# A mixture-of-experts layer: shared expert weights kept resident, one list product per step, and half a shared product moved behind the first up product

## The chip, the cores and the metric

The kernel runs on one core of one Trainium2 chip. The metric is the device time of one execution in microseconds. The engines are named as in the profile: PE (TensorE), DVE (VectorE), ACT (ScalarE), POOL (GpSimd), SP (SyncE, which here only issues DMAs). Each executes its own instructions in order and waits on semaphores.

## The reference

One decoder layer over 512 tokens of width 1024, everything in float32 unless the kernel lists token numbers. After the mixers and the output projection the residual stream is x. Then:

```
h2  = rmsnorm(x, g_ffn)
idx, wts = route(h2, w_router, router_bias)      # sigmoid scores, top 8 of 64, group-limited
moe = routed_experts(h2, idx, wts, w_exp_gate, w_exp_up, w_exp_down) \
    + swiglu(h2, w_sh_gate, w_sh_up, w_sh_down)  # the shared expert: 1024 -> 256 -> 1024
x   = x + moe
x   = x + sigmoid(rmsnorm(x, g_ple) @ w_ple_gate) * rmsnorm(p @ w_ple_proj, g_ple_post)
```

Each of the 64 experts has gate and up matrices of 1024x256 and a down matrix of 256x1024, 3 MB in all; the 64 together are 192 MB of the 301 MB that the kernel moves.

## The kernel before

The tokens are four tiles of 128. The first third of the kernel computes the mixers. The gates of the mixers lie in the buffer `gates`, whose upper half `hi` (8 KB a partition for the router's weights and more) is free once `merged_ready` has counted to 8. Weights go through `ring`, 12 slots of 1 MB.

In the middle stage (263 to 349 us in the trace) PE makes the output projection (`out_proj`), transposes x (`second_T`), computes the router's logits (`router`), and ranks each token among those of its expert (`rank`). DVE selects the experts (`select`) and builds `place`, bf16 one-hot matrices that say which token stands in which slot of an expert's list. ACT writes the normed rows h2 to HBM in four stores (line 900). POOL gathers them from there by the lists, 128 rows a step, with indirect DMAs (`gather`, line 759); it starts when the stores have landed (`act_moved`) and the first list is there (`rows_listed`).

The expert loop has `STEPS` = 40 steps of 128 slots. Experts are sorted by how many tokens they have and taken in groups of four: the first 8 groups have 96 slots an expert, so 3 steps a group, the other 8 have 64, so 2 steps. Step r does, on PE: `up(r)` (64 matmuls, line 2105), the transposes of the activations of r-1, the transposes of the gathered rows of r+1 (`rows_T`, line 1654), a round of lists `lists(r)` for the next groups as long as r < 16, jobs of the shared expert, and `down(r-1)` (line 2134). ACT and DVE each copy half of the transposed rows to `hgT` (lines 933 and 1472; for step 0 ACT copies both, lines 964 and 933), ACT applies silu (938), DVE multiplies (1477). The order in each engine's queue is the order in which the program is written.

A round of lists multiplies each 128x128 block of `place` by two small matrices in separate chains of matmuls: by `tokc` (token number, 2 columns, line 1987) and by `tokw` (weight in three bf16 parts and a rank for two experts, 8 columns, line 1994).

SP issues all weight loads in one order. A slot is loaded again when the product that reads it is done: `in_used(step)` waits for `gu_ps`, `down_used(step)` for `y_ps`. In a group of three steps the third up product frees two experts' gate and up slots at once. Expert 3's gate and up weights go to slots 6 and 7.

The shared expert is computed for tiles 0 and 1 in the middle stage (`shared_up`, line 1931, in pieces that fill PE's waits; the last piece, k = 4 to 8 of tile 1, stands behind `rows_T(0)` and ahead of `up(0)`), and for tiles 2 and 3 in steps 24 to 26 (`late_up`, lines 1917 and 1920). Its gate and up weights are loaded to slots 6 and 7 for the first two tiles, and again to `hi` and a piece of `lo`, the lower half of `gates`, for the other two (lines 547 and 549). Up product 1 writes the PSUM bank of tile 1's shared product, so it waits for `shared_act` to be 2.

Of the kernel before, what the change touches and what calls it, by code (L numbers as in the profile page):

```python
# [55 lines left out]
LCOL = TCOL + 2 * WCOL  # L56
# [76 lines left out]
def alibi_table():  # L133
# [17 lines left out]
    ["wa0", "wb0", "wa1", "wb1"] + [f"out{c}" for c in range(4)] + ["shg", "shu"]  # L151
DENSE_SLOT = [u % 8 for u in range(17)] + [1, 2, 3, 4, 6, 7]
# [25 lines left out]
def build(nc, t, y_dram, h2_dram, out):  # L178
    ctx = ExitStack()
    with ctx:  # L180
# [46 lines left out]
        prow = hi[:, 2 * D:3 * D].rearrange("p (i n) -> p i n", i=NT)  # L227
        rw = hi[:, 3 * D:3 * D + KD * NE].rearrange("p (k e) -> p k e", k=KD)
        gffn = hi[:, 0:D]
        sh_row = hi[:, 0:NT * FE].rearrange("p (i f) -> p i f", i=NT)  # L230
# [4 lines left out]
        lo3 = lo[:, 3 * D:4 * D]  # L235
        rows3 = rows[:, 3, :]
        shg_late = hi[:, 2 * D:4 * D].rearrange("p (k n) -> p k n", k=KD)
        shu_late = [w.rearrange("p (k n) -> p k n", k=KD // 2) for w in (lo3, hi[:, D:2 * D])]
        choice, masked, repl, gscr = (hi[:, D + k * NR:D + (k + 1) * NR] for k in range(4))
# [13 lines left out]
        WM = NR * WCOL // 2  # L253
# [13 lines left out]
        idT = sb("idT", [P, P], BF16)  # L267
# [48 lines left out]
        mid_loaded, late_loaded, sh_late_loaded = sem("mid_loaded"), sem("late_loaded"), sem("sh_late_loaded")  # L316
# [41 lines left out]
        def unit_source(name):  # L358

            w_in = t["w_in"][0].rearrange("(p k) n -> p k n", k=KD)  # L360
            c0 = {"q0": 512, "q1": 768, "kv": 1024, "pool0": 0, "pool1": 256}
            if name in c0:
                return w_in[:, :, c0[name]:c0[name] + 256]
            n = int(name[-1]) if name[-1].isdigit() else 0
            if name.startswith("gate"):
                return t["w_gate"][0].rearrange("(p k) n -> p k n", k=KD)[:, :, n * 256:(n + 1) * 256]
            if name[:2] in ("wa", "wb"):
                w = t["w_branch_a" if name[1] == "a" else "w_branch_b"][0]
                return w.rearrange("(k p) n -> p k n", p=P)[:, :, n * 512:(n + 1) * 512]
            if name.startswith("out"):  # L370
                return t["w_out"][0].rearrange("(k p) n -> p k n", p=P)[:, :, n * 256:(n + 1) * 256]
            if name == "shg":
                return t["w_sh_gate"][0].rearrange("(k p) n -> p k n", p=P)
            if name == "shu":
                return t["w_sh_up"][0].rearrange("(k p) n -> p k n", p=P)
            raise ValueError(name)
# [78 lines left out]
        def _(sp):  # L455
# [28 lines left out]
            for u in range(8, DENSE_AT["shg"]):  # L484
                load_dense(u)
# [3 lines left out]
            for u in range(DENSE_AT["shg"], N_DENSE):  # L489
                load_dense(u)  # L490
# [4 lines left out]
            sp.dma_start(rbias, t["router_bias"].broadcast_to([P, NE])).then_inc(mid_loaded, 16)  # L495

# [339 lines left out]
        def _(act):  # L836
# [187 lines left out]
        def _(dve):  # L1024
# [33 lines left out]
            nc.vector.tensor_copy(idT[:, :], cst[:, C_ID:C_ID + P])  # L1058
# [253 lines left out]
            nc.vector.tensor_copy(tokc[:, :, 1], cst[:, C_TILE:C_TILE + NT])  # L1312
            residual(0, 0)
# [98 lines left out]
            link(nc.vector.tensor_copy(tw3[:, :, 0], r_w))  # L1412
            link(nc.vector.tensor_tensor(rest, r_w, tw3[:, :, 0], ALU.subtract))
            link(nc.vector.tensor_copy(tw3[:, :, 1], rest))
            link(nc.vector.tensor_tensor(rest, rest, tw3[:, :, 1], ALU.subtract))
            nc.vector.tensor_copy(tw3[:, :, 2], rest)
# [10 lines left out]
            nc.vector.tensor_scalar(tokw[:, :, :, 3], count_of[:, b, :, HEAD:], -1.0, None, ALU.add  # L1427
                                    ).then_inc(tokw_ready, 1)
            shared_mult(1)


            def weights_of(g, found):
# [4 lines left out]
                w = found[:, :, TCOL:].rearrange("p s (e c) -> p s e c", e=2)  # L1437
# [72 lines left out]
            for r in range(STEPS):  # L1510
                if r:
                    act_T(r - 1, (r - 1) % 2)
                act_rows(r, r % 2)
                if r + 1 < STEPS:
                    rows_T(r + 1, (r + 1) % 2)
                if 1 <= r < NGROUP:
                    dve.wait_ge(list_ps, r + 1)
                    rows_of(r, found_of(r))
                    if r == 1:
                        weights_of(0, found_of(0))  # L1520
                    weights_of(r, found_of(r))
                    if r + 1 < NGROUP:
                        places(r + 1, rank3[:, :, (r + 1) * GROUP:(r + 2) * GROUP])
                for n in jobs_of(r, 0) + jobs_of(r, 1):
                    if n < 6 and n % 3 < 2:
                        late_T(n // 3, n % 3)
                    elif n < 6:
                        shared_mult(LATE[n // 3])
                    elif n < 8:
                        shared_T(n - 6)  # L1530
                    elif n < 8 + 2 * NT:
                        base(n - 8)
                    else:
                        ple_gain(n - 8 - 2 * NT)
# [107 lines left out]
        def _(pe):  # L1642
# [267 lines left out]
            def late_up(c):  # L1910

                i = LATE[c]
                pe.wait_ge(sh_late_loaded, 48)
                pe.wait_ge(h2T_ready, 2 * NT + 2 * c + 2)
                for k in range(KD):
                    xT = xT_late[k // 4][:, k % 4, :]
                    mm(bank(5)[:, 0:FE], xT, shg_late[:, k, :], start=(k == 0), stop=(k == KD - 1))
                for k in range(KD):
                    xT = xT_late[k // 4][:, k % 4, :]
                    last = mm(bank(5)[:, FE:2 * FE], xT, shu_late[k // 4][:, k % 4, :], start=(k == 0),  # L1920
                              stop=(k == KD - 1))
                last.then_inc(shared_ps, 1)

            def shared_up(i, k0, k1):

                if i == 0 and k0 == 0:
                    loaded("shg")
                    loaded("shu")
                w = pair_view(DENSE_SLOT[DENSE_AT["shg"]])
                for k in range(k0, k1):  # L1930
                    last = mm(bank(SH_BANK[i]), actT[:, k, i * P:(i + 1) * P], w[:, k], start=(k == 0),  # L1931
                              stop=(k == KD - 1))
# [52 lines left out]
            def list_rows(g, at, s):  # L1985
                for i in range(NT):
                    last = mm(at, place[:, g % 2, i, s * P:(s + 1) * P], tokc[:, i, :], start=(i == 0),
# [3 lines left out]
            def list_weights(g, at, s):  # L1991
# [7 lines left out]
            for s in range(steps_of(0)):  # L1999
                last = list_rows(0, bank(5)[:, 328 + s * TCOL:328 + (s + 1) * TCOL], s)  # L2000
# [20 lines left out]
            def lists(g):  # L2021
# [3 lines left out]
                if g == 1:  # L2025
                    pe.wait_ge(tokw_ready, 1)
                    for s in range(steps_of(0)):
                        list_weights(0, bank(5)[:, s * LCOL + TCOL:(s + 1) * LCOL], s)
                else:
                    pe.wait_ge(list_ready, g)  # L2030
                for s in range(steps_of(g)):
                    at = (g % 2) * 64 + s * LCOL
                    list_rows(g, bank(5)[:, at:at + TCOL], s)
                    last = list_weights(g, bank(5)[:, at + TCOL:at + LCOL], s)
# [154 lines left out]
            def o_products(e, n, j):  # L2189
                pe.wait_ge(o_over, n + 1)  # L2190
                pe.wait_ge(o_place_ready, n + 1)
                for i in range(NT):
                    mm(bank(5)[0:CAP, 0:TCOL], o_place[:, i, :], tokc[:, i, :], start=(i == 0), stop=(i == NT - 1))
                for i in range(NT):
                    last = mm(bank(5)[0:CAP, TCOL:TCOL + WCOL], o_place[:, i, :],
# [94 lines left out]
```

## Time and profile before

| what | value |
|---|---|
| runs | 996.63, 996.40, 994.88 us; median 996.4 |
| the profiled execution | 995.38 us, its span 993.5 us |
| busy in the span | PE 941.1 us (95%), DVE 339.4 (34%), ACT 162.6 (16%), POOL 201.4 (20%) |
| matmuls | 6263 |
| DMA | 301.03 MB, mean 303 GB/s |
| expert loop | 349 to 903 us |

The span is the time from the first to the last instruction that the profiler recorded; the rest of the execution's time lies around it. "PE busy" includes time in which a pipelined matmul's end is modelled. PE's granted clock is 0.98 to 1.00 of full speed through most of the expert loop.

### The profile page before, as it was taken

The numbers are of one execution on the slowest core, as the hardware profiler recorded it, in microseconds if no ns is written. First come the engines' busy times: TensorE is split into PE (matmuls) and PEld (weight loads), VectorE is DVE, ScalarE is ACT, GpSimd is POOL, SyncE is SP. The second block draws the span as 40 slices with busy tenths as digits, with TensorE's granted clock in tenths as the row PEclk, the third lists the DMA queues.
The fourth block names the chain that finished last, engine by engine and source line by source line (L and its number), as shares of the span: only waits on it lengthen the run. The fifth ranks groups of instructions, "written<-read, shape, count | busy, mean of one in ns | idle before, by whom it ended". The sixth has DMA issues, their size and how long they took to land.

```text
span 993.5 us, 15496 instructions
## 1 busy us (share of the span) xinstructions
PE 941.1 (95%) x6263; PEld 465.7 (47%) x6263; DVE 339.4 (34%) x749; ACT 162.6 (16%) x304; POOL 201.4 (20%) x332
## 2 busy tenths in 40 slices
PE   6999999999999999999999999999979898997698
PEld 4578888854446533333333333354323332332344
DVE  5565673222226753333332111111101111111687
ACT  2001334120011211111111111111101112121021
POOL 4115923000010102222222222212121211101210
PEclk9999999999999999999999999999989999999799
DMA  9940002265362599999999999999999999999972
GB/s 331 326 128 1 1 1 85 85 201 180 105 288 75 195 385 373 410 416 401 393 418 415 414 419 414 410 423 415 405 422 422 422 420 421 414 400 361 368 274 84
DMA packets 83911, 301.03 MB, mean 303 GB/s; under 512 B 9299, under 2 KB 35959, under 8 KB 59648
## 3 DMA queue, kind: packets, MB, share of 16 engines
q1 hardware_dynamic: 71200, 264.24, 67.7%
q0 software_dynamic: 11920, 33.63, 8.7%
q10 hardware_dynamic: 720, 2.16, 0.5%
q8 instruction: 50, 0.82, 0.3%
q14 instruction: 21, 0.17, 0.0%
HBM read 279.26 MB, written 29.36 MB: 311 GB/s over the span
## 4 chain that ended last, share of the span: by engine, by line
PE 76%; DMA 18%; DVE 2%; SPq 2%; issue 1%; ACT 1%; DVEq 0%; POOL 0%; ACTq 0%
PE ps L2105 22%; DMA ring<-in_w_exp_up 16%; PE ps L1721 12%; PE ps L2134 9%; PE ps L1860 6%; PE ps L2247 5%; PE ps L1677 3%; PE ps L1844 3%; PE ps L1842 3%; PE ps L1654 2%; DMA ring<-in_w_exp_down 2%; PE ps L1931 1%; PE ps L1683 1%; PE ps L2114 1%; SPq L514 1%; SPq L500 1%
## 5 line engine op out<-in xcount | busy, mean ns | idle before, releaser
L2105 PE MATMUL ps<-ring,gates 128*32 128x512 f32 x2560 | 288.8, 603 | 26.1 <-DMA ring<-in_w_exp_up 25.4
L2105 PEld LDWEIGHTS ps<-ring,gates 128*32 128x32 f32 x2560 | 87.6, 111 | 219.0 <-issue 218.1
L2134 PE MATMUL ps<-ring,poolbuf 128*32 128x512 f32 x1280 | 147.3, 601 | 3.0 <-DMA ring<-in_w_exp_down 2.1
L1482 DVE COPY poolbuf<-ps 128x256 f32<-128x256 f32 x40 | 17.0, 424 | 356.2 <-PE ps L2114 356.2
L747 POOL TENSOR_TENSOR tickets<-cst 128x1 f32<-128x1 f32 x77 | 14.5, 188 | 398.2 <-ACT actT L946 392.7
L2134 PEld LDWEIGHTS ps<-ring,poolbuf 128*32 128x32 f32 x1280 | 38.3, 110 | 84.7 <-issue 83.0
L946 ACT ACTIVATE actT<-ps,qT 128x1024 f32<-128x1024 f32 x40 | 44.5, 1113 | 143.9 <-PE ps L2134 143.9
L938 ACT ACTIVATE poolbuf<-ps 128x256 f32<-128x256 f32 x40 | 15.3, 384 | 279.3 <-PE ps L2105 279.3
L1721 PE MATMUL ps<-xrow,ring 128*128 128x256 f32 x256 | 57.9, 381 | 0.1
L1860 PE MATMUL ps<-ring,gates 128*128 128x512 f32 x128 | 56.4, 594 | 0.0
L1654 PE MATMUL ps<-cst,rows 128*128 128x128 f32 x352 | 48.5, 285 | 7.6 <-DVE rows L1035 7.6
L1721 PEld LDWEIGHTS ps<-xrow,ring 128*128 128x128 f32 x256 | 48.3, 190 | 8.0 <-issue 1.2
L1654 PEld LDWEIGHTS ps<-cst,rows 128*128 128x128 f32 x352 | 44.7, 193 | 9.5 <-issue 8.9
L1721 PE MATMUL ps<-actT,ring 128*128 128x256 f32 x208 | 47.5, 381 | 0.0
L688 POOL TENSOR_SCALAR st<-st 128x1 f32<-128x1 f32 (+2 forms) x17 | 6.7, 393 | 196.2 <-ACT rows L891 135.3
L759 POOL DMA_INDIRECT rows<-h_rows,stage x40 | 41.8, 1045 | 21.4 <-issue 19.0
L764 POOL DMA_INDIRECT accumulator<-actT,stage x40 | 40.6, 1016 | 22.1 <-issue 22.1
L2247 PE MATMUL ps<-ring,actT 128*128 128x512 f32 (+1 forms) x112 | 42.2, 531 | 0.0
L1721 PEld LDWEIGHTS ps<-actT,ring 128*128 128x128 f32 x208 | 39.0, 190 | 6.7 <-issue 1.4
L720 POOL TENSOR_TENSOR ring<-ring 128x1024 f32<-128x1024 f32 x12 | 28.3, 2361 | 52.4 <-DMA ring<-in_w_gate 30.3
L1860 PEld LDWEIGHTS ps<-ring,gates 128*128 128x128 f32 x128 | 23.8, 190 | 27.3 <-issue 27.3
L2247 PEld LDWEIGHTS ps<-ring,actT 128*128 128x128 f32 x112 | 20.9, 190 | 18.0 <-issue 17.2
(269 smaller groups left out, 1001.3 us busy)
## 6 DMA issues: line engine op xcount, KB each, us to landing
ring<-in_w_exp_down SPq DMA_DIRECT2D x64, 1024.0 KB
ring<-in_w_exp_gate SPq DMA_DIRECT2D x62, 1024.0 KB, 10.8
ring<-in_w_exp_up SPq DMA_DIRECT2D x62, 1024.0 KB, 18.9
ring<-accumulator SPq DMA_DIRECT2D x12, 1024.0 KB, 12.5
ring<-in_w_gate SPq DMA_DIRECT2D x8, 1024.0 KB, 10.1
ring<-in_w_in SPq DMA_DIRECT2D x5, 1024.0 KB, 13.0
xrow<-in_x SPq DMA_DIRECT2D x8, 512.0 KB, 7.5
accumulator<-ring SPq DMA_DIRECT2D x1, 4096.0 KB, 19.6
```

What stands on the lines that cost most here:

```text
L759: pool.indirect_dma_start(hg[j], None, h2_dram, bass.IndirectOffsetOnAxis(ap=stage[:, 0, j, :], axis=0), bounds_check=T - 1, oob_is_err=Fa ...
L764: pool.indirect_dma_start(y_dram, bass.IndirectOffsetOnAxis(ap=stage[:, 1, j, :], axis=0), yrow[j], None, bounds_check=ACC_ROWS - 1, oob_i ...
L946: nc.scalar.activation(yrow[j], bank(6, 2), ACT.Copy, scale=slot_wr[:, r, 0:1]).then_inc(y_ready, 1)
L1654: last = nc.tensor.transpose(bank(b0 + half)[:, k * width:(k + 1) * width], v[0:width, 4 * half + k, :], ident[0:width, 0:width])
L1677: last = mm(bank(2 * (i % 2)), actT[:, k, i * P:(i + 1) * P], qv[:, k], start=(k == 0), stop=(k == KD - 1))
L1721: last = mm(out[:, f * HALF_T:(f + 1) * HALF_T], w[:, k, f * P:(f + 1) * P], x[:, k, :], start=(k == 0), stop=(k == 3))
L1842: mm(bank(b), wa[:, k, mi * P:(mi + 1) * P], mixedT[:, k, :], start=(k == 0), stop=(k == 3))
L1844: last = mm(bank(b + 1), wb[:, k, mi * P:(mi + 1) * P], qT[:, k, :], start=(k == 0), stop=(k == 3))
L1860: last = mm(bank(half), gates[:, k, i * P:(i + 1) * P], w[:, k], start=(k == 0), stop=(k == KD - 1))
L2105: last = mm(bank(2 + k)[part, :], hgT[k][:, q, part], pair_view(EXPERT_SLOT[js[c]])[:, q], start=(q == 0), stop=(q == KD - 1))
L2134: last = mm(bank(6 + half)[part, :], eactT[r % 2][:, q, part], w[:, q, half * 512:(half + 1) * 512], start=(q == 0), stop=(q == 1))
L2247: last = mm(gate_bank(i, n0)[:, 0:width], xT, unit_view(s, 4)[:, k % 4, n0 % 512:n0 % 512 + width], start=(k == 0), stop=(k == KD - 1))
```

## The change

The shared expert's gate and up weights are loaded once, to all of `hi` (`w_sh`), behind the middle loads and ahead of the first experts; all four tiles read them from there. The middle stage's small tensors (`gffn`, `prow`, `rw` and the scratch of the selection) move from `hi` to ring slots 6 and 7. Expert 3's gate half is loaded when those in slot 6 have been read, its up half when those in slot 7 have. `tokw` gets six columns an expert, the token number's two ahead of the four, so a round of lists is one chain of matmuls with 12 columns (`list_all`). The token columns are filled by two copies on DVE. `late_up` uses one chain of 512 columns instead of two of 256. The last piece of tile 1's shared product stands behind `up(0)` on PE; its silu stands behind that of step 0 on ACT, its product behind that of step 0 on DVE, where it stood at the end of the weights' calculation. The load of `w_ple` waits for it as well, and an unused bf16 identity is not made.

```diff
-LCOL = TCOL + 2 * WCOL
+ECOL = TCOL + WCOL
+LCOL = 2 * ECOL
...
-        gffn = hi[:, 0:D]
+        gffn = ring[:, 6, 0:D]
+        prow = ring[:, 6, D:2 * D].rearrange("p (i n) -> p i n", i=NT)
+        rw = ring[:, 7, 0:KD * NE].rearrange("p (k e) -> p k e", k=KD)
+        w_sh = hi.rearrange("p (u k n) -> p k u n", u=2, k=KD)
...
-            for u in range(DENSE_AT["shg"], N_DENSE):
-                load_dense(u)
             sp.wait_ge(merged_ready, KD)
             sp.dma_start(gffn, t["g_ffn"].broadcast_to([P, D])).then_inc(mid_loaded, 16)
...
+            for u, name in enumerate(("w_sh_gate", "w_sh_up")):
+                sp.dma_start(w_sh[:, :, u, :], t[name][0].rearrange("(k p) n -> p k n", p=P)
+                             ).then_inc(shared_loaded, 16)
...
             load_in(2, 2)
+            sp.dma_start(gpost, t["g_ple_post"].broadcast_to([P, D])).then_inc(late_loaded, 16)
+            sp.wait_ge(xg_ready, 2 * NT)
+            sp.wait_ge(pT_ps, 2)
+            load_part(3, 3, 0)
             sp.wait_ge(logit_ps, NT)
-            sp.wait_ge(pT_ps, 2)
-            sp.wait_ge(sel_ready, NT)
-            sp.wait_ge(gathered[0], 16)
-            sp.dma_start(shg_late, unit_source("shg")).then_inc(sh_late_loaded, 16)
-            for c in range(2):
-                sp.dma_start(shu_late[c], unit_source("shu")[:, 4 * c:4 * c + 4, :]).then_inc(sh_late_loaded, 16)
-            sp.dma_start(gpost, t["g_ple_post"].broadcast_to([P, D])).then_inc(late_loaded, 16)
-            sp.wait_ge(shared_ps, 2)
-            load_in(3, 3)
+            sp.wait_ge(masked_ready, 2)
+            load_part(3, 3, 1)
...
                 sp.wait_ge(tokw_ready, 1)
+                sp.wait_ge(shared_ps, 2)
...
-            shared_silu_of(1)
             for r in range(STEPS):
                 silu(r, r % 2)
+                if r == 0:
+                    shared_silu_of(1)
...
-            nc.vector.tensor_copy(idT[:, :], cst[:, C_ID:C_ID + P])
...
+            nc.vector.tensor_copy(tokw[:, :, :, 0],
+                                  cst[:, C_PM:C_PM + 1].unsqueeze(1).broadcast_to([P, NT, NE]))
+            nc.vector.tensor_copy(tokw[:, :, :, 1],
+                                  cst[:, C_TILE:C_TILE + NT].unsqueeze(2).broadcast_to([P, NT, NE]))
...
-            shared_mult(1)
...
                 act_rows(r, r % 2)
+                if r == 0:
+                    shared_mult(1)
...
                 for k in range(KD):
-                    xT = xT_late[k // 4][:, k % 4, :]
-                    mm(bank(5)[:, 0:FE], xT, shg_late[:, k, :], start=(k == 0), stop=(k == KD - 1))
-                for k in range(KD):
-                    xT = xT_late[k // 4][:, k % 4, :]
-                    last = mm(bank(5)[:, FE:2 * FE], xT, shu_late[k // 4][:, k % 4, :], start=(k == 0),
-                              stop=(k == KD - 1))
+                    last = mm(bank(5), xT_late[k // 4][:, k % 4, :], w_sh[:, k], start=(k == 0), stop=(k == KD - 1))
...
-                    list_rows(g, bank(5)[:, at:at + TCOL], s)
-                    last = list_weights(g, bank(5)[:, at + TCOL:at + LCOL], s)
+                    last = list_all(g, s)
...
             rows_T(0)
-            shared_up(1, 4, 8)
             for r in range(STEPS):
                 up(r)
+                if r == 0:
+                    shared_up(1, 4, 8)
```

## Rows read from the trace of the kernel before

**Rows 1.** The page, part 4: the chain that ended last, by engine.

```profile
PE 76%; DMA 18%; DVE 2%; SPq 2%; issue 1%; ACT 1%; DVEq 0%; POOL 0%; ACTq 0%
```

**Rows 2.** Stretches: start:end, length, busy per engine (instructions), clock, DMA share, GB/s.

```profile
378.20:415.40 37.20, 37.20 (x391) 14.75 (x391) 13.63 (x45) 6.22 (x10) 8.48 (x18) 1.00 0.99 399
415.40:452.40 37.00, 37.00 (x392) 14.64 (x391) 13.07 (x45) 6.28 (x10) 8.48 (x18) 1.00 1.01 410
452.40:488.90 36.50, 36.50 (x369) 14.14 (x369) 11.68 (x45) 6.38 (x10) 8.47 (x18) 1.00 1.01 409
488.90:525.20 36.30, 36.30 (x367) 13.94 (x367) 11.68 (x45) 6.18 (x10) 8.48 (x18) 1.00 0.99 401
525.20:561.30 36.10, 36.10 (x353) 13.65 (x353) 8.66 (x35) 6.37 (x10) 8.47 (x18) 1.00 1.01 416
...
500.00:526.00 26.00, 26.00 (x261) 10.46 (x254) 8.35 (x32) 4.57 (x7) 5.65 (x12) 1.00 1.01 421
```

**Rows 3.** The same view, slices of 1 us where the DMA falls off.

```profile
380.00:381.00 1.00, 1.00 (x13) 0.36 (x16) 0.81 (x7) 0.07 (x1) 0.00 (x0) 1.00 0.72 270
454.00:455.00 1.00, 1.00 (x12) 0.26 (x8) 0.83 (x7) 0.11 (x1) 0.00 (x0) 1.00 0.69 233
490.00:491.00 1.00, 1.00 (x19) 0.46 (x19) 0.92 (x6) 0.51 (x1) 0.00 (x0) 1.00 0.66 225
...
702.00:703.00 1.00, 1.00 (x13) 0.83 (x15) 1.00 (x4) 0.45 (x1) 0.00 (x0) 1.00 0.77 274
```

**Rows 4.** SP's timeline: start, us, what it issues.

```profile
343.42 0.38 SPq L547 DMA_DIRECT2D gates<-in_w_sh_gate  x1
...
350.45 0.44 SPq L500 DMA_DIRECT2D ring<-in_w_exp_up  x1
```

**Rows 5.** The chain of waits from 345 to 393 us: start, us, what.

```profile
345.01 0.89 PE ps L1654 x8
...
349.34 7.13 PE ps L2105 x64
...
358.17 7.08 PE ps L2105 x64
...
391.79 0.08 PE ps L1987 x4
391.87 0.10 PE ps L1994 x4
...
392.38 3.57 PE ps L2134 x32
```

**Rows 6.** DVE's timeline; in brackets the idle time before and what ended it.

```profile
269.97 0.69 DVE L1231 TENSOR_TENSOR xrow<-xrow,ps 128x512 f32<-128x512 f32 x1 [4.70 <-PE ps L1860]
...
353.99 0.45 DVE L1389 SCALAR_TENSOR_TENSOR gates<-ps,st,gates 128x256 f32<-128x256 f32 x1
...
357.24 0.68 DVE L1472 COPY gates<-ps 128x512 f32<-128x512 f32 x1
```

**Rows 7.** ACT's timeline.

```profile
332.31 0.33 ACTq L900 DMA_DIRECT2D h_rows<-rows  x1
...
345.98 0.59 ACT L933 ACTIVATE gates<-ps 128x512 f32<-128x512 f32 x1
349.38 0.48 ACT L926 ACTIVATE gates<-ps,st 128x256 f32<-128x256 f32 x1 [2.80 <-PE ps L1931]
```

**Rows 8.** DMA issues, stores at 281.75, 295.40, 332.31: KB, us to landing.

```profile
h_rows<-rows ACTq DMA_DIRECT2D x1, 512.0 KB, 8.0
...
h_rows<-rows ACTq DMA_DIRECT2D x1, 512.0 KB, 2.6
...
h_rows<-rows ACTq DMA_DIRECT2D x1, 512.0 KB, 3.7
```

**Rows 9.** POOL's timeline: the first gather.

```profile
338.80 1.19 POOL L759 DMA_INDIRECT rows<-h_rows,stage  x1 [0.86 <-POOL stage L752]
```

**Rows 10.** Line 759, all 40 gathers: issue to landing.

```profile
DMA to landing us min/median/max: 4.7/10.1/11.6
```

More of the change, by code:

```diff
@@ L150 @@
 DENSE = ["q0", "q1", "kv", "pool0", "pool1"] + [f"gate{p + h * PAIRS}" for p in range(PAIRS) for h in range(2)] + \
-    ["wa0", "wb0", "wa1", "wb1"] + [f"out{c}" for c in range(4)] + ["shg", "shu"]
-DENSE_SLOT = [u % 8 for u in range(17)] + [1, 2, 3, 4, 6, 7]
+    ["wa0", "wb0", "wa1", "wb1"] + [f"out{c}" for c in range(4)]
+DENSE_SLOT = [u % 8 for u in range(17)] + [1, 2, 3, 4]
 DENSE_AT = {name: n for n, name in enumerate(DENSE)}
@@ L226, in build @@
         pp = hi.rearrange("p (i n) -> p i n", i=NT)
-        prow = hi[:, 2 * D:3 * D].rearrange("p (i n) -> p i n", i=NT)
-        rw = hi[:, 3 * D:3 * D + KD * NE].rearrange("p (k e) -> p k e", k=KD)
-        gffn = hi[:, 0:D]
-        sh_row = hi[:, 0:NT * FE].rearrange("p (i f) -> p i f", i=NT)
+        gffn = ring[:, 6, 0:D]
+        prow = ring[:, 6, D:2 * D].rearrange("p (i n) -> p i n", i=NT)
+        rw = ring[:, 7, 0:KD * NE].rearrange("p (k e) -> p k e", k=KD)
+        w_sh = hi.rearrange("p (u k n) -> p k u n", u=2, k=KD)
+        sh_row = lo[:, 3 * D:4 * D].rearrange("p (i f) -> p i f", i=NT)
         sh_act = hi[:, 2 * T:4 * T].rearrange("p (j n) -> p j n", j=2)
@@ L234, in build @@
         NR = NT * NE
-        lo3 = lo[:, 3 * D:4 * D]
         rows3 = rows[:, 3, :]
-        shg_late = hi[:, 2 * D:4 * D].rearrange("p (k n) -> p k n", k=KD)
-        shu_late = [w.rearrange("p (k n) -> p k n", k=KD // 2) for w in (lo3, hi[:, D:2 * D])]
-        choice, masked, repl, gscr = (hi[:, D + k * NR:D + (k + 1) * NR] for k in range(4))
+        choice, masked, repl, gscr = (ring[:, 7, KD * NE + k * NR:KD * NE + (k + 1) * NR] for k in range(4))
         key_row, above, perm = (poolbuf[0:NE, PL + k * NE:PL + (k + 1) * NE] for k in range(3))
@@ L252, in build @@
         ka = kT[:, :, :].rearrange("p a n -> p (a n)")
-        WM = NR * WCOL // 2
+        WM = NR * ECOL // 2
         tokw = ka[:, 0:WM].bitcast(BF16).rearrange("p (i e c) -> p i e c", i=NT, e=NE)
@@ L266, in build @@
         oneT = sb("oneT", [P, P], BF16)
-        idT = sb("idT", [P, P], BF16)
         order = vecs[0:1, 0:NE].bitcast(U32)
@@ L315, in build @@
         x1_ps, x1_ready = sem("x1_ps"), sem("x1_ready")
-        mid_loaded, late_loaded, sh_late_loaded = sem("mid_loaded"), sem("late_loaded"), sem("sh_late_loaded")
+        mid_loaded, late_loaded, shared_loaded = sem("mid_loaded"), sem("late_loaded"), sem("shared_loaded")
         ssq2_done, rstd2_ready, xg_ready, h2_ready, act_moved = (
@@ L371, in unit_source @@
                 return t["w_out"][0].rearrange("(k p) n -> p k n", p=P)[:, :, n * 256:(n + 1) * 256]
[L372 to L375, printed above, removed]
             raise ValueError(name)
@@ L483, in _ @@
             sp.dma_start(y_rows[0], zero_row.unsqueeze(1).broadcast_to([P, TOPK, D])).then_inc(y_first, 16)
-            for u in range(8, DENSE_AT["shg"]):
+            for u in range(8, N_DENSE):
                 load_dense(u)
@@ L1411, in _ @@
             tw3 = tokw.rearrange("p i e c -> p (i e) c")
[L1412 to L1416, printed above, removed]
+            link(nc.vector.tensor_copy(tw3[:, :, TCOL], r_w))
+            link(nc.vector.tensor_tensor(rest, r_w, tw3[:, :, TCOL], ALU.subtract))
+            link(nc.vector.tensor_copy(tw3[:, :, TCOL + 1], rest))
+            link(nc.vector.tensor_tensor(rest, rest, tw3[:, :, TCOL + 1], ALU.subtract))
+            nc.vector.tensor_copy(tw3[:, :, TCOL + 2], rest)
             for b in range(2):
@@ L1426, in _ @@
                 b, span = 1 - b, 2 * span
-            nc.vector.tensor_scalar(tokw[:, :, :, 3], count_of[:, b, :, HEAD:], -1.0, None, ALU.add
+            nc.vector.tensor_scalar(tokw[:, :, :, TCOL + 3], count_of[:, b, :, HEAD:], -1.0, None, ALU.add
                                     ).then_inc(tokw_ready, 1)
-            shared_mult(1)
             def weights_of(g, found):
@@ L1436, in weights_of @@
                 r = slice(FIRST_STEP[g], FIRST_STEP[g] + n)
-                w = found[:, :, TCOL:].rearrange("p s (e c) -> p s e c", e=2)
+                w = found.rearrange("p s (e c) -> p s e c", e=2)[:, :, :, TCOL:]
                 own = cst[:, C_PAIR:C_PAIR + 6] if g < BIG_GROUPS else cst[:, C_PAIR2:C_PAIR2 + 4]
@@ L1926, in shared_up @@
                 if i == 0 and k0 == 0:
-                    loaded("shg")
-                    loaded("shu")
-                w = pair_view(DENSE_SLOT[DENSE_AT["shg"]])
+                    pe.wait_ge(shared_loaded, 32)
                 for k in range(k0, k1):
-                    last = mm(bank(SH_BANK[i]), actT[:, k, i * P:(i + 1) * P], w[:, k], start=(k == 0),
+                    last = mm(bank(SH_BANK[i]), actT[:, k, i * P:(i + 1) * P], w_sh[:, k], start=(k == 0),
                               stop=(k == KD - 1))
@@ L1983, in _, with first_rows, list_all @@
             shared_up(0, 6, 7)
-            def list_rows(g, at, s):
+            def first_rows(at, s):
                 for i in range(NT):
-                    last = mm(at, place[:, g % 2, i, s * P:(s + 1) * P], tokc[:, i, :], start=(i == 0),
+                    last = mm(at, place[:, 0, i, s * P:(s + 1) * P], tokc[:, i, :], start=(i == 0),
                               stop=(i == NT - 1))
                 return last
-            def list_weights(g, at, s):
+            def list_all(g, s):
+                at = bank(5)[:, (g % 2) * 64 + s * LCOL:(g % 2) * 64 + (s + 1) * LCOL]
                 e = g * GROUP + pair_of(g, s)
@@ L1999, in _ @@
             for s in range(steps_of(0)):
-                last = list_rows(0, bank(5)[:, 328 + s * TCOL:328 + (s + 1) * TCOL], s)
+                last = first_rows(bank(5)[:, 328 + s * TCOL:328 + (s + 1) * TCOL], s)
             last.then_inc(list_ps, 1)
@@ L2027, in lists @@
                     for s in range(steps_of(0)):
-                        list_weights(0, bank(5)[:, s * LCOL + TCOL:(s + 1) * LCOL], s)
+                        list_all(0, s)
                 else:
@@ L2192, in o_products @@
                 for i in range(NT):
-                    mm(bank(5)[0:CAP, 0:TCOL], o_place[:, i, :], tokc[:, i, :], start=(i == 0), stop=(i == NT - 1))
-                for i in range(NT):
-                    last = mm(bank(5)[0:CAP, TCOL:TCOL + WCOL], o_place[:, i, :],
+                    last = mm(bank(5)[0:CAP, 0:ECOL], o_place[:, i, :],
                               tokw[:, i, bass.ds(e, 1), :].rearrange("p e c -> p (e c)"),
```

3 lines of the change are left out of this document (removed).

## Prediction, made before the changed kernel was run

> **What bounds the kernel now.** I read the page first: TensorE is busy for 941 us of a span of 993.5, yet the chain that ended last is 76% PE and 18% DMA [rows 1]. So two resources take turns, and the question is where each one holds the end. The next view was the busy time by stretches. The expert loop runs 40 steps, from 349 to 903 us; its first 24 steps take three steps to a group of four experts, the other 16 take two. From 378 to 561 us PE is busy in every microsecond, and the DMA moves 399 to 416 GB/s by stretches of three steps; in the best piece, from 500 to 526, it moves 421 [rows 2]. I take 421 as what it can do.
>
> The reader should turn the first five stretches into dry time. 37.2 us at 399 GB/s are 14.84 MB, which at 421 take 35.3 us, so 1.9 us were not used; the next four give 1.0, 1.0, 1.7 and 0.4. Even the last of these, in which no single slice falls far, loses 0.4, so I call 0.45 the floor and get 1.45, 0.55, 0.55, 1.25 and 0 of real drought. Narrow slices show where it lies: 270 GB/s at 380, 233 at 454, 225 at 490 [rows 3], and a weaker one near 416. Each is the moment at which the third step of a group ends and SP gets four slots at once: just before it, the queue had run empty. After 492 there is no such hole before 702, where PE's own chain is the longer one again [rows 3]. So up to 489 us the end moves with PE's progress, and from there with bytes only. That is the frame of every term below: **what counts is by how much PE ends its 12th up product (489 us) earlier or later.**
>
> **Part by part.** (1) *Bytes and order of the loads.* The second load of the shared weights (2 MB, with the wait for the first gather ahead of it) goes; 2 MB of expert 3, issued at 349.62 behind two halves of shared product, are now issued when the gained rows and the masked weights are ready. Before, these and 0.5 MB of gain made a backlog from 343.4 on [rows 4]. It was gone by 380, where the DMA falls to 270 GB/s [rows 3]. Expert 3 is first wanted by the third up product, 12.9 us after the second (358.17 [rows 5]), and its 2 MB, last issued at 350.45 [rows 4], need 5 us at 421 GB/s behind at most 2.5 MB of the others; the late shared weights are wanted 300 us later. Nobody waited for either, and the queue ran empty behind them, so I price the removed and advanced bytes at 0. The other end of that price is all 4.2 MB at 421 GB/s, 10 us, if something later than 381 still carried the backlog.
>
> (2) *Load order at 263 to 270.* The first copy of the shared weights (one load at 235, one at 263) moves behind the middle loads, ahead of the first experts; 2 MB at 421 GB/s push experts 0 and 1 back by 5 us. They are wanted at 349; cost 0, the cover is 50 us long. Two added copies on DVE fill the token columns. The nearest row, a product of 128x256, is 0.45 us, and DVE is idle for 4.70 us right behind that place [rows 6]: 0. The identity copy that goes is one small copy near the start, on a DVE that PE doesn't wait for there: 0, at most 0.2.
>
> (3) *Lists: one chain of matmuls for two.* Second list round: 36 matmuls become 24. The six others of large groups: 24 become 12. The eight of small groups: 16 become 8. In the chain, a round of 24 lies between 391.79 and the down product at 392.38: 0.59 us, 24.5 ns each [rows 5]. Columns hardly matter: four with 2 columns take 0.08 us, four with 8 columns 0.10 [rows 5], so one of 12 should take what one of 8 does. Up to the release at 489 the lists of steps 1 to 10 count: 12+72+24 = 108 matmuls, 2.65 us. The 40 of steps 11 to 15 (1.0 us) come when bytes decide, and give nothing. Bounds: 0 saved if time went by columns (12 against 2+8), 3.6 if all came through.
>
> The Trainium skill (TensorE: Matmul & The Clock Gate, section LDWEIGHTS) has a weight load take its columns over 1.2 per ns, 107 ns for these 128. If pairs were spaced by that, 148 removed pairs would give 15.8 us; the spacing of 24.5 ns here does not agree, so I give it no chance, and the sum goes by the row.
>
> (4) *The half product behind the first up product.* Before, PE ends the transposes of rows 0 at 345.90, runs the half product for 3.44 us (to 349.34), then up product 0 for 7.13, and starts up product 1 at 358.17, 12.27 us later [rows 5]. The half product hid two ACT copies of the transposed rows, the second of which ends at 345.98+0.59 = 346.57 [rows 7]. Now: up product 0 can start at 346.57 plus 0.25 (the gap from DVE's copy, 357.24+0.68, to PE at 358.17 [rows 5, 6]) = 346.8, and ends at 353.95. The half product ends at 357.4. Meanwhile ACT's silu and DVE's product of step 0 are done under it. What is late next is the chain for bank 3 and for the next rows: ACT's shared silu 0.48 [rows 7], DVE's shared product 0.45, and then, queued behind it on DVE, the copy of the next transposed rows 0.68 [rows 6], with 0.25 to PE: 357.4+0.5+0.45+0.68+0.25 = 359.3. So up product 1 starts **1.1 us later** than 358.17. Bounds: 0 if the new hole in front of step 0 doesn't open, 2 if the waits on both engines add up. SP's loads of the PLE projection now wait for the shared product too, to 357.4; they stood behind up product 0 (356.47) already, and behind them on SP stands only a wait for up product 1: 0.
>
> (5) *The first gather.* One new wait comes from traffic. The store of the last h2 rows is issued by ACT at 332.31 [rows 7]. With expert 2's load in flight to about 335.5 it took 3.7 us; the first such store, at 281.75 in a long backlog, took 8.0, the second with none 2.6 [rows 8]. Now SP puts the 0.5 MB gain behind expert 2's load, then expert 3's gate half at about 330.3, which keep the DMA busy for 1.57 MB/421 = 3.7 us more, to about 339, and the up half at 336.6, to 341.5. If the store lands when the backlog before it has drained, as I read the first one, it is there at 339 instead of 336. POOL starts the gather at 338.80 [rows 9], and wants the store 1 us before. The gather would start near 340 and land near 345 instead of by 343.4 (SP's wait for it ended there, where the late shared load is issued [rows 4]); PE can use it from about 344.5, half a microsecond ahead of 345.01. I take **0.4 us**; bounds 0 and 4.4: a gather takes 10.1 us in the median, nearly all of them under full load, 4.7 at best [rows 10], so 338.80+10.1 = 348.9 against 344.5.
>
> The Trainium skill (DMA: Bandwidth & Descriptors, Queues, rings and completion order) says that each engine goes round the queues packet by packet. By this the store would get half the rate, 0.5 MB more or 1.25 us over 2.6, landing at 336.2, and this term would be 0. The store of 8.0 us does not agree with an equal share.
>
> **Sum**, at the release at 489: +1.1 +0.4 -2.65 = -1.15 us. The check is whether the DMA can follow. At the release at 378 the shift is +1.1+0.4-0.3 = +1.2, so between 378 and 489 PE gains 2.35 us on the DMA, and the drought at 416, 454 and 490 is 0.55+0.55+1.25 = 2.35. It just can. From there to the end nothing changes: the product of tiles 2 and 3 in one chain of 512 columns has the same columns as two of 256, and behind the DMA's load that follows 702 it would not show. The profiled execution took 995.38 (span 993.5 and 1.9 around it), 1.0 under the median of 996.4. So 994.2 for it, and **995.3** for the median.
>
> **Rivals.** *Bytes decide earlier than I think* (chance 0.10). The DMA is over 98% busy in every stretch from 378 on, and 4.2 MB less ahead of it would bring 5 to 10 us: 986 to 991. Against it stands that the queue empties four times behind the removed bytes. *All of PE's gain comes through* (0.10): the floor of 0.45 us a group is real drought too, the lists of steps 11 to 15 then count, -3.6+1.5 = -2.1: 994.3. *Wider lists cost what the narrow ones did* (0.10): +1.1+0.4 = +1.5: 997.9. *The early load of expert 3 sits on the way to the first gather* (0.15): place, the transposes of rows 0, with no half product left behind them to work on; price up to 4.4 instead of 0.4, so +2.9: 999.3. It turns the sum to slower once the gather lands more than 1.55 us behind 344.5, at 346. For it speak the store of 8.0 us and the gathers' 10.1 under load; against it that only 1 MB is left in the queue when the gather starts. The forecast itself has 0.55, with -0.3 to -2.0.
>
> **From cases to numbers.** This kernel's measurement tells 0.2%, 2 us, from no change, so the forecast lies inside. Faster by more: 0.09 of the bytes, 0.06 of the full gain and 0.11 of the forecast's edge, 0.26. Slower by more: 0.11 of the gather, 0.03 of the wide lists and 0.05 of the forecast's edge, 0.19. No change: 0.55. The range runs from 992.8 (full gain, and runs that lie 1.5 below the median as one of the three did) to 998.3 (wide lists, or half of the gather's price).
>
> **What would show it.** Rounds of lists in the chain with 12 and 8 matmuls, 0.29 and 0.20 us. Up product 0 starting near 347, a hole of 0.9 us or more ahead of it, up product 1 near 359.3+0.4 and up product 11 ending near 487.4. Dips of the DMA still there near 452 and 489, but shallower. I am wrong if the first gather lands after 346, if the DMA no longer dips at all after 380 and the time falls by 5 us, or if PE at 489 has moved and the landing at 653 has not.

## The result

The changed kernel takes 999.97 us in the median of 14 runs, against 996.18 of 14 runs of the kernel before. The ratio is 1.0040, with a 95% interval of 1.0031 to 1.0048: slower by 3.8 us. The profiled execution took 1002.39 us (span 1000.5). It was the slowest of the 14, so the trace shows 3 us more than the medians do, and I go by medians for sizes and by the trace for places.

The page after, parts 1 and 4. PE has 180 matmuls and 2.4 us of busy time less, the DMA 2.1 MB less (298.91 MB). The share of PE in the chain fell from 76% to 69%, that of the DMA rose from 18% to 25% [rows 1].

```profile
PE 938.7 (94%) x6083; PEld 457.0 (46%) x6083; DVE 340.6 (34%) x750; ACT 162.9 (16%) x304; POOL 202.4 (20%) x332
...
PE 69%; DMA 25%; SPq 2%; DVE 2%; issue 1%; ACT 1%; DVEq 0%; POOL 0%; ACTq 0%; POOLq 0%
```

SP's timeline after, from 328 to 337 us: the gain, then expert 3's gate half and its up half. All three are issued before the first gather.

```profile
328.37 0.43 SPq L538 DMA_DIRECT2D gates<-in_g_ple_post  x1
330.28 0.33 SPq L495 DMA_DIRECT2D ring<-in_w_exp_gate  x1
336.54 0.33 SPq L495 DMA_DIRECT2D ring<-in_w_exp_up  x1
```

The chain of waits after, from 332 us. Before, it ran through PE alone here (345.01, 349.34, 358.17 in [rows 5]).

```profile
332.29 9.07 DMA h_rows<-rows
...
342.47 4.57 DMA rows<-h_rows,stage
...
347.08 1.59 PE ps L1652 x8
348.68 0.73 issue
349.41 9.56 PE ps L2093 x64
358.97 3.65 PE ps L1920 x8
...
364.28 7.08 PE ps L2093 x64
```

The store of the last h2 rows took 9.07 us instead of 3.7 [rows 8]; it landed at 341.36. The gather started at 342.47 instead of 338.80 [rows 9], took no longer than before, and the transposes of rows 0 started at 347.08 instead of 345.01. The reader should then look at the durations: the eight transposes took 1.59 us instead of 0.89, and up product 0 took 9.56 instead of 7.13. The stretches say why (columns as in [rows 2]; the last two are the DMA's busy share and GB/s):

```profile
336.00:337.00 1.00, 1.00 (x15) 0.44 (x13) 0.66 (x4) 0.00 (x0) 0.00 (x0) 1.00 1.04 393
...
341.00:342.00 1.00, 1.00 (x9) 0.91 (x9) 0.00 (x0) 0.82 (x2) 0.19 (x1) 1.00 0.96 393
342.00:343.00 1.00, 1.00 (x10) 0.95 (x9) 0.00 (x0) 0.00 (x0) 0.53 (x1) 1.00 0.49 205
...
345.00:346.00 1.00, 0.00 (x1) 0.00 (x0) 0.97 (x3) 0.00 (x0) 0.97 (x2) 1.00 0.79 307
346.00:347.00 1.00, 0.00 (x0) 0.00 (x0) 0.96 (x3) 0.00 (x0) 0.26 (x1) 1.00 0.64 119
347.00:348.00 1.00, 0.92 (x6) 0.92 (x7) 0.86 (x5) 0.14 (x1) 0.76 (x1) 0.82 0.59 209
349.00:350.00 1.00, 0.59 (x4) 0.23 (x8) 0.96 (x2) 0.31 (x1) 0.00 (x0) 0.50 0.46 164
```

The DMA queue is busy without a break until 342, so it had not emptied when the up half was issued at 336.54; the store landed at 341.36, as it ran out. PE did nothing for 2.1 us, from 345.0 to 347.1. Behind it the granted clock (the third column from the end) reads 0.82 at 347 and 0.50 at 349, the lower of its two levels, 1.2 GHz.

### The profile page after: what moved, and what is told of

The parts are those of the page before. It is cut to its first block, busy times and chain, and to the rows that moved or that the text cites. A ratio compares the mean times of both kernels' runs of the same rounds, so it can differ in the third digit from the quotient of the medians.

```text
span 1000.5 us, 15133 instructions
## 1 busy us (share of the span) xinstructions
PE 938.7 (94%) x6083; PEld 457.0 (46%) x6083; DVE 340.6 (34%) x750; ACT 162.9 (16%) x304; POOL 202.4 (20%) x332
## 2 busy tenths in 40 slices
DMA packets 81815, 298.91 MB, mean 299 GB/s; under 512 B 9252, under 2 KB 33864, under 8 KB 57553
## 4 chain that ended last, share of the span: by engine, by line
PE 69%; DMA 25%; SPq 2%; DVE 2%; issue 1%; ACT 1%; DVEq 0%; POOL 0%; ACTq 0%; POOLq 0%
DMA ring<-in_w_exp_up 21%; PE ps L2093 20%; PE ps L1719 12%; PE ps L2122 7%; PE ps L1858 6%; PE ps L2234 5%; PE ps L1675 3%; PE ps L1842 3%; PE ps L1840 3%; DMA ring<-in_w_exp_down 2%; PE ps L1652 2%; PE ps L1912 1%; PE ps L1681 1%; SPq L509 1%; SPq L495 1%
## 5 line engine op out<-in xcount | busy, mean ns | idle before, releaser
L752 POOL DMA_INDIRECT rows<-h_rows,stage x40 | 42.0, 1051 | 21.3 <-issue 18.9
L926 ACT ACTIVATE gates<-ps 128x512 f32<-128x512 f32 x40 | 23.9, 597 | 32.5 <-PE ps L1652 32.5
```

Of the source, the lines that this page charges most:

```text
L752: pool.indirect_dma_start(hg[j], None, h2_dram, bass.IndirectOffsetOnAxis(ap=stage[:, 0, j, :], axis=0), bounds_check=T - 1, oob_is_err=Fa ...
```

## Experiments

Where the loop stands is best read from the starts of up products, taken from each kernel's PE timeline (us, one execution each). The last three columns are that execution's time, the median of all runs, and the ratio to the kernel before in the same session, with its 95% interval. The changed kernel was measured in one session, e1 to e4 in a second, e5 to e8 in a third and e9 to e11 in a fourth, so kernels of different sessions are better compared by their ratios (0.0010 is 1.0 us) than by their medians. Single executions of one kernel lie up to 2.6 us from their median in this table, so its middle columns show places and not the worth at the end.

| kernel | up 1 | up 3 | up 11 ends | up 16 | up 25 | traced | median | ratio |
|---|---|---|---|---|---|---|---|---|
| before | 358.2 | 383.4 | 488.6 | 542.2 | 653.6 | 995.4 | 996.2 | |
| changed | 364.3 | 388.7 | 492.6 | 547.6 | 662.1 | 1002.4 | 1000.0 | 1.0040 (1.0031 to 1.0048) |
| e1 loads behind the gather | 359.2 | 383.6 | 487.0 | 544.3 | 656.1 | 997.8 | 997.5 | 1.0010 (0.9998 to 1.0022) |
| e2 half product ahead | 362.8 | 387.2 | 490.3 | 546.1 | 659.6 | 1001.7 | 1000.7 | 1.0041 (1.0026 to 1.0057) |
| e3 both | 358.0 | 382.4 | 485.5 | 542.3 | 653.4 | 993.4 | 996.0 | 0.9999 (0.9989 to 1.0010) |
| e4 lists only | 358.1 | 382.6 | 485.6 | 542.6 | 656.6 | 997.7 | 995.7 | 1.0000 (0.9990 to 1.0010) |
| e5 wait filled | 361.0 | 385.6 | 488.7 | 544.5 | 658.8 | 1000.5 | 999.4 | 1.0025 (1.0013 to 1.0037) |
| e6 loads behind the store | 364.8 | 389.2 | 492.3 | 547.6 | 663.2 | 1004.5 | 1002.5 | 1.0056 (1.0036 to 1.0076) |
| e7 extra PE work, step 3 | 358.1 | 383.1 | 490.8 | 544.8 | 660.3 | 1000.7 | 999.9 | 1.0024 (1.0009 to 1.0038) |
| e8 extra PE work, step 13 | 358.2 | 383.2 | 488.4 | 544.6 | 655.0 | 993.6 | 995.7 | 0.9993 (0.9983 to 1.0003) |
| e9 2.9 MB less | 358.1 | 383.1 | 488.2 | 541.9 | 653.3 | 993.8 | 994.2 | 0.9980 (0.9969 to 0.9991) |
| e10 2.9 MB less, lists | 358.1 | 382.5 | 485.6 | 538.3 | 650.4 | 993.7 | 992.6 | 0.9960 (0.9946 to 0.9974) |
| e11 gate half early | 359.7 | 384.1 | 487.2 | 542.7 | 654.9 | 995.9 | 996.9 | 1.0009 (0.9993 to 1.0026) |

**e1: the early loads behind the first gather.**

```diff
-            sp.dma_start(gpost, ...)
             sp.wait_ge(xg_ready, 2 * NT)
             sp.wait_ge(pT_ps, 2)
-            load_part(3, 3, 0)
             sp.wait_ge(logit_ps, NT)
             sp.wait_ge(masked_ready, 2)
-            load_part(3, 3, 1)
+            sp.wait_ge(gathered[0], 16)
+            load_in(3, 3)
+            sp.dma_start(gpost, ...)
```

> The changed kernel with expert 3's two loads and the 0.5 MB gain put back behind the landing of the first gather; nothing else differs. Theory G (traffic on the way to the first gather, with the clock that PE loses while it waits): the last h2 store lands near 336 instead of 341.4, the first gather by 343.5, the transposes of rows 0 start at 345.0, up product 0 takes 7.1 us instead of 9.6, and up product 1 starts near 359.3 instead of 364.3; the time falls by 4 to 5 us from 1000.0, to 995 to 996. Theory H (the half product behind up product 0 is what costs): PE's order is unchanged, so 998.5 to 1000. Theory D (the DMA-bound part of the expert loop is slower because fewer bytes lie ahead of it or the lists are shorter): the start improves by 5 us and the end by 1 or less, 999.

Measured 997.5, below the changed kernel by 2.5 us by the medians and 3.0 by the ratios: most of the loss goes, so Theory H is out as the main cause. Theory G had asked for 995 to 996; the 5.1 us that it gave for up product 1 came (359.2 instead of 364.3), but not all of it at the end. The chain of waits of e1, in which step 0 is as I had worked it out for the prediction (346.8, 353.95, 359.3):

```profile
345.18 0.45 PE ps L1652 x4
...
345.65 0.61 ACT gates L957
346.26 0.58 issue
346.84 7.07 PE ps L2093 x64
353.91 3.65 PE ps L1920 x8
...
358.09 0.48 DVE gates L1386
358.57 0.61 DVE gates L1468
```

**e2 and e3: the half product ahead of up product 0 again**, in the changed kernel and in e1.

```diff
             rows_T(0)
+            shared_up(1, 4, 8)
             for r in range(STEPS):
                 up(r)
-                if r == 0:
-                    shared_up(1, 4, 8)
```

> The changed kernel with the half product of tile 1 back ahead of up product 0, and its silu and product back in their old places on ACT and DVE. Theory G: the first gather is as late as in the changed kernel (landing near 347), and the clock drops all the same; only the 0.9 us hole ahead of up product 0 goes, so 998 to 999.5. Theory H: the whole loss goes, 995 to 996.5. Theory D: 999 to 1000.

> The changed kernel with both edits of the two kernels before: expert 3 and the gain loaded behind the first gather, and the half product ahead of up product 0. What is left of the change is the resident shared weights and the single chain of matmuls in the lists. Theory G: up product 0 starts at 349.3 and up product 1 at 358.2 as before the change, the lists bring up to 2.65 us: 993.5 to 994.5. Theory D: the end does not follow, 996 to 999.

e2 is at 1000.7, no better than the changed kernel and above the 998 to 999.5 of Theory G. Its gather is as late, and now the half product takes the loss of clock: 4.97 us instead of 3.44 (the chain of e2):

```profile
332.24 9.81 DMA h_rows<-rows
...
343.16 4.45 DMA rows<-h_rows,stage
...
348.95 4.97 PE ps L1918 x8
```

e3 is at 996.0, below e1 by 1.5 us by the medians and 1.1 by the ratios, and level with the kernel before. So the half product costs about 1 us where the gather is in time (the intervals of e1 and e3 still overlap, so its worth at the end is likely and not shown) and nothing visible where it is late. And e3 still has the resident weights and the short lists, of which nothing is left in the time: that is Theory D's side of the expectation.

**e4: the lists alone** in the kernel before.

```diff
-                    list_rows(g, bank(5)[:, at:at + TCOL], s)
-                    last = list_weights(g, bank(5)[:, at + TCOL:at + LCOL], s)
+                    last = list_all(g, s)
```

> The kernel before the change with nothing but the lists' single chain of 12 columns (and the two copies that fill the token columns). My count of the prediction: rounds of 0.29 and 0.20 us instead of 0.59 and 0.39, 2.6 us by the release at 489, 993.5 to 994.5. Theory D, in its form that shorter steps only uncover a load-bound loop: up products start earlier by 2 us until 489, then PE waits for loads, and the end moves by less than 1 us, 995.5 to 996.5, or is later.

995.7, ratio 1.0000. The matmuls do go: up product 11 ends at 485.6 instead of 488.6. But up product 12 starts at 493.1 instead of 493.6. The chain of e4 there, and its stretches:

```profile
474.47 18.46 DMA ring<-in_w_exp_up
492.92 0.14 issue
493.06 8.77 PE ps L2109 x64
```

```profile
490.00:492.00 2.00, 0.71 (x8) 0.00 (x0) 0.23 (x1) 1.11 (x1) 0.00 (x0) 1.00 1.02 414
492.00:494.00 2.00, 0.94 (x8) 0.43 (x12) 0.00 (x0) 0.00 (x0) 1.31 (x3) 0.80 1.00 420
494.00:496.00 2.00, 2.00 (x15) 0.58 (x11) 0.00 (x0) 0.00 (x0) 1.33 (x4) 0.50 1.01 410
```

A load of the next group, issued when up product 10 ended, took 18.5 us; PE could have taken it at 490.5 (where e10 starts up product 12), which leaves it 16.0. PE waits 2.4 us (from 490.7 to 493.06), the granted clock falls to half, the product takes 8.77 us instead of 7.1. The same load took 18.9 us in e1, but 14.8 in e3, where up product 12 starts at 490.4 without a wait. There the wait comes later (e3's PE timeline):

```profile
528.67 8.77 PE L2091 MATMUL ps<-ring,gates 128*32 128x512 f32 x64 [2.28 <-DMA ring<-in_w_exp_up]
```

By up product 16 e3 and e4 both stand where the kernel before stands, at 542.2 to 542.6. So the lead is lost at one place or another within four steps; what decides at which is not shown.

**e5: PE's wait filled.**

```diff
+            pe.wait_ge(ssq2_done, NT)
+            for _ in range(2):
+                mm(bank(1), ident, actT[:, 0, :], start=True, stop=True)
             rows_T(0)
```

> The changed kernel with two extra matmuls of 128x512 (1.7 us, their result is not used) between the last piece of shared product ahead of the loop and PE's wait for the first gather. The gather stays as late as it is, near 347; only the time in which PE idles shrinks from 2.1 to 0.4 us. Theory C (the late gather costs twice, once as the wait and once as the clock that PE loses by idling): the clock stays at 1.00, the transposes take 0.9 us instead of 1.6, up product 0 7.1 instead of 9.6, up product 1 starts near 361.2 instead of 364.3, and the time falls by 2 to 3 us, to 997 to 998. If the clock falls in spite of it, or if loads bound the loop anyway, 999.5 to 1000.

The chain of e5:

```profile
344.98 1.72 PE ps L2141 x4
346.70 0.72 PE ps L1652 x4
...
348.64 7.07 PE ps L2093 x64
...
361.02 7.07 PE ps L2093 x64
```

On the spot Theory C is right: the gather's wait is nearly closed, the clock stays up, up product 1 starts 3.3 us earlier than in the changed kernel. The end gains 0.6 us by the medians (999.4) and 1.5 by the ratios (1.0025 and 1.0040), less than the 2 to 3 that I expected of C; their intervals leave room for anything from nothing to 3 us. The loss of clock at the first step is shown; what it costs at the end is not settled.

**e6 and e11: when the early loads are issued.** e6 puts `sp.wait_ge(act_moved, 16 + 16 * NT)` ahead of the gain and both halves, so the last store has landed before they start; e11 keeps the gate half where the change has it and puts the gain and the up half behind the gather.

> The changed kernel with the gain and expert 3's two loads issued when the four h2 stores have landed, so that they are in flight with the first gather and not with the last store. Theory S (the store is what the loads delay; a gather beside 2.5 MB of loads shares evenly): store landed by 336, gather started at 338.8 and landed by 345, time as with these loads behind the gather, 997.5. Theory Q (any transfer of another queue that starts behind a backlog lands only when the backlog is nearly drained): the loads run from 338 to 344.5, the gather lands at 345.5 to 347, PE waits 1 to 2 us and loses its clock, 999 to 1000.5.

> The changed kernel with only expert 3's gate half (1 MB) loaded ahead of the first gather, as in the change; the gain and the up half wait for the gather. The backlog at the last h2 store is 1 MB longer than before the change instead of 1.5 MB plus 1 MB more. If the store lands when the backlog has drained (Theory Q), it lands at 337.5 to 338.5, the gather by 344.5 to 345, PE waits less than 0.5 us and keeps its clock, up product 0 takes 7.1 us: 997 to 998, as with no early load. If any load that overlaps the store costs its full delay, 998.5 to 999.5.

The chains of e6, then of e11:

```profile
339.03 8.53 DMA rows<-h_rows,stage
347.60 1.37 PE ps L1653 x8
348.97 0.73 issue
349.70 9.80 PE ps L2094 x64
```

```profile
332.50 7.19 DMA h_rows<-rows
340.01 0.79 issue
340.80 4.54 DMA rows<-h_rows,stage
345.38 0.72 PE ps L1653 x4
...
347.31 7.07 PE ps L2094 x64
```

In e6 the store is back at 3.9 us, and the gather beside 2.5 MB of loads takes 8.53 instead of 4.5. PE waits 2.4 us, loses its clock, and the kernel is the slowest of all, 1002.5. On the spot Theory Q holds for both kinds of transfer. Its time, 999 to 1000.5, missed by 2 us: up product 1 starts only 0.5 us later than in the changed kernel, and why the end is 1.6 us later by the ratios, if it is (the intervals overlap), is open. In e11 the store took 7.2 us (I had said 5 to 6), the gather landed at 345.3, PE waited 0.2 us, and the time is 996.9, by the ratios (1.0009 and 1.0010) that of e1. So 1 MB of early load fits, 2.5 MB do not.

**e7 and e8: 2.6 us more work for PE**, in step 3 and in step 13 of the kernel before (r == 4 and r == 14 in `rows_T`).

```diff
+                if r == 4:
+                    for _ in range(3):
+                        mm(bank(1), ident, xrow[:, 3, 0:512], start=True, stop=True)
                 strided_T(hg[j], None, 0, P, hgT_ps)
```

> The kernel before the change with three extra matmuls of 128x512 (2.6 us, their result is not used) on PE in step 3, ahead of the transposes of rows 4. By the prediction's frame (up to 489 us the end moves with PE's progress) the end moves by nearly all of it, 998.3 to 998.8. By Theory D (the loop is bound by loads; PE's lead or lag in the first 12 steps is taken up by when its loads land) it moves by less than 1 us, 996 to 997.

> The same three extra matmuls in step 13 instead, behind the point at which the prediction has the DMA take over. By the prediction's frame nothing moves, 995.8 to 996.6, as by Theory D; if PE's progress decides throughout the large groups, 998.3 to 998.8 as in step 3.

In step 3 it costs 2.4 us by the ratio (3.5 by the medians), in step 13 nothing (0.9993, 0.9983 to 1.0003). That is the prediction's frame in the direction of a delay.

**e9 and e10: 2.9 MB of loads left out**, in the kernel before and in e4. The down matrices of three experts are loaded in 128 of their 2048 columns only, and the down products use old values in the others.

```diff
                     down_used(step)
-                    load_down(pos, e[0])
+                    (load_down_part if g <= 3 else load_down)(pos, e[0])
```

> The kernel before the change with three of the down loads (first expert of groups 1 to 3, issued between 371 and 445 us) cut to a sixteenth of their columns, so 2.9 MB or 7 us of DMA time are left out and those experts' down products use old values. By the prediction's frame (the DMA runs dry up to 489, so bytes ahead of it are worth nothing) the time stays, 995.5 to 996.5. By Theory E (from about 390 on, PE and the DMA are within a microsecond or two of each other, and the loads for the next group land just when they are wanted) a lead of the DMA carries over to the bytes-bound part: 989 to 993.

> The same cut of 2.9 MB in the kernel that has nothing of the change but the single list chain. If the lists' gain was lost because loads landed too late for the shorter steps (Theory E), it shows now, at least in part: 1.5 to 2.6 us below the run with the cut alone. If the lists' matmuls save PE nothing that counts in any case, it equals that run.

e9 gains 2.0 us by the ratio, though all the bytes left out lie ahead of 489; it falls short of Theory E's 3 to 7. e10 gains 4.0: with bytes out of the way, up product 12 starts at 490.5 (493.1 in e4), up product 16 at 538.3 (542.6), and the lists are worth 1.6 to 2.0 us where alone they were worth 0 (the difference of the medians and of the two ratios; the intervals of the ratios overlap at their ends, 0.9969 to 0.9974).

## Why the prediction was wrong

The sum said -1.15 us, the kernel lost 3.8; 999.97 lies above the range. In the sum's own terms, read from the ratios, +1.1 (half product), +0.4 (first gather) and -2.65 (lists) came out as about +1.1 (e1 against e3), +3.0 (changed kernel against e1) and 0 (e4). Two terms failed, the gather's and the lists'. Step by step:

- **Step 5, the first gather: mis-sized, 0.4 us taken, 2.1 measured, and its second price was missing.** The mechanism was named: store behind the backlog, gather behind the store, no half product left to cover it. The error is in the drain. I had the up half in flight to 341.5 and let the store land at 339, when the backlog "before it" would be gone; but the up half is issued at 336.54, before the queue has emptied, and the store landed at 341.36. Behind the wait of 2.1 us came 0.7 us of slow transposes and 2.4 of a slow up product, which I had priced at 0: PE's granted clock was 0.82 and 0.50 behind the wait. Up product 1 started 6.1 us late instead of 1.5. I also counted the cost from 344.5, though PE is busy with a piece of the shared product until 345.0 in both kernels. This was the fourth rival, 0.15, with 999.3. Its place was right; that its number is near is in part luck, for it had 4.4 us of pure waiting and still took the lists' 2.65 off.
- **The price of the clock could be read before.** In the kernel before, PE waits for a load ahead of up product 25 and then takes 8.77 us for it; the second line is e7's, where the clock stays at 1.00:

```profile
653.59 8.77 PE L2105 MATMUL ps<-ring,gates 128*32 128x512 f32 x64 [2.23 <-DMA ring<-in_w_exp_up]
660.30 7.07 PE L2108 MATMUL ps<-ring,gates 128*32 128x512 f32 x64 [2.82 <-DMA ring<-in_w_exp_up]
```

  So a wait of 2 to 3 us may cost a second time, and need not.
- **Its worth in the end**: changed against e1 2.5 us by the medians and 3.0 by the ratios, against e11 3.1. The place of the loss is shown. Against the kernel before, the lag shrinks from 6.1 us at up product 1 to 4.0 at the end of 11, since the short lists give PE time back (3.0 us by then in e4). Against e1, which has the same lists, it is 5.1 at up product 1, 5.6 at the end of 11 and 3.3 at 16: ahead of up product 12 e1 waits 2.8 us for a load and runs that product in 8.77 us, and the changed kernel doesn't wait there. A part of being early is lost in such waits; how much of the 5 us reaches the end is known only from the medians.
- **Step 4, the half product: right.** Predicted 1.1, e1 shows up product 1 at 359.2 against 358.2; at the end about 1 us.
- **Step 3, the lists: right on PE, wrong at the end.** A round of 12 matmuls takes 0.28 us (the chain after; predicted 0.29):

```profile
385.03 0.28 PE ps L1984 x12
385.32 3.57 PE ps L2122 x32
```

  and in e4 up product 11 ends 3.0 us earlier. The end doesn't move (e3, e4). It is the last of the signs that the prediction names: PE at 489 has moved (485.5 in e3 against 488.6), the landing ahead of up product 25 has not (it starts at 653.4 against 653.6). What failed is the check that "the DMA just can follow": I counted all of the DMA's dips up to 490 as capacity that a faster PE would use. A dip says that the queue ran empty before a release; it doesn't say that the one load for which PE will wait next arrives sooner. That load was 18.5 us on the way in e4, longer than the two short steps leave. e10 supports it: with 2.9 MB less the lists count.
- **The frame** (PE decides to 489, bytes behind it) holds for a delay of 2.6 us (e7 +2.4, e8 0) and not for gains (e3, e4, e9). In the large groups PE with the short lists needs 35.8 to 36.2 us for three steps, and the DMA 34.6 to 36.0 for their bytes at 421 GB/s (an estimate from the stretches of [rows 2]), so a lag passes at least in part to the end, and a lead runs into the other.
- **Steps 1 and 2, the bytes: right for the change itself.** e3, with resident weights and 2.1 MB less, is level with e4 and the kernel before. In the changed kernel the DMA stands idle at 370 to 372 (the stretch after), where it moved 430 GB/s before:

```profile
370.00:372.00 2.00, 2.00 (x22) 0.86 (x14) 0.16 (x1) 0.39 (x1) 0.00 (x0) 1.00 0.00 0
```

  That bytes ahead of 489 are worth nothing anywhere was too wide, as e9 shows: 2.9 MB taken out at 371 to 445 bring 2 us of their 7.
- **The other reading of the queues.** The Trainium skill (DMA: Bandwidth & Descriptors, Queues, rings and completion order) has an engine go round its queues packet by packet. An equal share would have put the store at 336.2; with 1 to 2.5 MB more of loads issued around it the 0.5 MB took 7.2 to 9.8 us, and 3.8 with only expert 2's. No run here shows what the packets do inside; as a rule for when a small transfer lands beside a loaded queue, the drained backlog was the better one.

What stays open: why e2, with up product 1 1.5 us earlier than the changed kernel, ends no earlier, why e5 with 3.3 gains only 0.6 to 1.5, and why e6 ends later than the changed kernel. In all of them the loop meets loads that land late, and one trace a kernel doesn't show how often.

No version that loads everything beat the kernel before. e3 keeps the resident weights and 2.1 MB less traffic at no cost that the runs show, and is the one to build on.

## What to carry to other kernels

Before a load is moved into an idle stretch of the DMA, look for the small transfer on the critical path that lives from that idleness (here a 0.5 MB store and then a gather), and count the queue that it will meet with everything issued before it has drained, not only before it starts. Give a new wait of PE of 2 to 3 us two prices, the wait alone and the wait with slow matmuls behind it (here 1.3 to 2.7 us more on a product of 7.1), and let the range hold both. Where PE and the DMA are within a few per cent of each other, forecast delays at up to their full price and gains at nothing until a run says otherwise.

## What was not expected of the hardware

A store of 0.5 MB took 2.6 us alone and 8.7 to 9.8 (e5, changed, e2) beside 2.5 MB of loads that another queue had issued before and after it; a gather of 128 rows took 4.5 and 8.5. In each of these the slowed transfer landed as the queue ran empty.

PE's granted clock stayed at 1.00 over idle times of 0.8 us (e1, e5, e11) and stood at 0.50 behind 2.1, 2.4, 2.7 and 2.4 us (changed, e6, e2, e4). The length of the wait alone does not decide it: ahead of other up products it stayed at 1.00, with the product at 7.1 us, over waits of 2.1 (changed, up 15), 2.5 (e11, up 15), 2.8 (e7, up 25) and 2.9 us (e2, up 15), while a wait of 2.0 us (e4, up 25) was followed by a product of 8.77. What else decides is not shown.
